# Bias rows written once and copied in memory; the last two expert tiles and the final norm by token half

## What is computed

```python
def second_block(x, c, ...):                       # x is the first block's output
    mod = (silu(c) @ w_mod + b_mod)                # 6 x 1024: sh1, sc1, gt1, sh2, sc2, gt2
    h = rmsnorm(x, ln_mix_g) * (1 + sc1) + sh1
    ...                                            # attention with a relative bias:
    s = einsum('bqgrd,bngd->bgrqn', qb, kc) + head_bias(t[:, None] - cmp_end)
    ...
    x = x + gt1 * (mixed @ w_out)
    h2 = rmsnorm(x, ln_ffn_g) * (1 + sc2) + sh2
    x = x + gt2 * peer_ffn(h2, peer_wq, peer_keys, peer_u, peer_v)
    return rmsnorm(x, ln_final_g)
```

## Time and profile before

| | |
|---|---|
| median of three runs | 1329.93 us (1328.16 to 1331.64) |
| profiled execution, its own time | 1328.11 us |
| its span | 1326.2 us |
| TensorE matmul busy | 1229.8 us, 93% |
| VectorE, ScalarE, GpSimd busy | 884.4, 771.6, 562.4 us |
| mean granted TensorE clock | 0.973 |
| moved by DMA | 249.36 MB, 188 GB/s |

### The profile page before, as it was taken

The page is one execution under the profiler, slowest core; times in us unless marked ns, Lnnn a source line. Parts: engine busy times, 40 slices in busy tenths (PEclk is TensorE's granted clock), DMA queues, the critical chain, the costliest instruction groups (busy, mean ns, idle before and its releaser), DMA issues.

```text
span 1326.2 us, 27600 instructions
## 1 busy us (share of the span) xinstructions
PE 1229.8 (93%) x8788; PEld 1124.6 (85%) x8788; DVE 884.4 (67%) x1750; ACT 771.6 (58%) x1719; POOL 562.4 (42%) x501
## 2 busy tenths in 40 slices
PE   7698988988898898999999999999999999999996
PEld 6587877877796677999999999999988878888885
DVE  4377858879735644799447777773086867676765
ACT  5233576544545544655678887886555555555554
POOL 2454445353325733698886777777700000000000
PEclk8899999999998989999999999999999999999998
DMA  5666655575452433455555656566666565757552
GB/s 212 123 223 196 204 199 185 192 259 185 150 209 105 150 97 125 148 186 177 172 175 183 192 187 197 189 191 207 241 200 253 195 240 195 259 191 254 192 196 87
DMA packets 86032, 249.36 MB, mean 188 GB/s; under 512 B 8275, under 2 KB 29907, under 8 KB 85196
## 3 DMA queue, kind: packets, MB, share of 16 engines
q1 hardware_dynamic: 77212, 209.69, 47.7%
q0 software_dynamic: 8752, 38.80, 9.1%
HBM read 235.36 MB, written 13.11 MB: 187 GB/s over the span
## 4 chain that ended last, share of the span: by engine, by line
PE 76%; DVE 9%; ACT 5%; DMA 4%; issue 3%; POOL 2%; DVEq 0%; ACTq 0%; SPq 0%
PE psum L639 75%; DMA ring<-weights 2%; DVE s_sb L1580 2%; POOL arena L1512 2%; ACT w_hi L1081 1%; DMA arena<-mods 1%; DVE w_lo L1571 1%; DVE arena L1805 1%; PE psum L817 1%; ACT arena L1222 1%; DMA ring<-v_rows 1%; DVE rstd L1565 1%; DVE arena L1673 0%; DMA par<-params 0%; DVE h_lo L1608 0%
## 5 line engine op out<-in xcount | busy, mean ns | idle before, releaser
L1081 ACT ACTIVATE w_hi<-ring 128x512 fp32r<-128x512 f32 x734 | 444.6, 627 | 299.5 <-PE psum L639 271.6
L1438 POOL TENSOR_TENSOR w_lo<-ring,w_hi 128x512 fp32r<-128x512 f32 x367 | 480.9, 1320 | 304.6 <-ACT w_hi L1081 292.1
L639 PE MATMUL psum<-h_hi,w_hi 128*128 128x256 f32 x1832 | 538.0, 294 | 50.7 <-DVE w_lo L1571 16.3
L639 PE MATMUL psum<-h_lo,w_hi 128*128 128x256 f32 x1832 | 523.2, 286 | 0.0
L639 PE MATMUL psum<-h_hi,w_lo 128*128 128x256 f32 x1832 | 522.5, 285 | 0.0
L639 PEld LDWEIGHTS psum<-h_hi,w_hi 128*128 128x128 f32 x1832 | 355.8, 194 | 69.8 <-ACT arena L1064 33.4
L639 PEld LDWEIGHTS psum<-h_lo,w_hi 128*128 128x128 f32 x1832 | 356.5, 195 | 0.2
L639 PEld LDWEIGHTS psum<-h_hi,w_lo 128*128 128x128 f32 x1832 | 356.0, 194 | 0.0
L1571 DVE TENSOR_TENSOR w_lo<-ring,w_hi 128x512 fp32r<-128x512 f32 x239 | 181.0, 757 | 144.0 <-ACT w_hi L1081 143.8
L639 PE MATMUL psum<-w_hi,h_hi 128*128 128x512 f32 (+1 forms) x592 | 223.9, 378 | 6.9 <-DVE arena L1588 5.6
L639 PE MATMUL psum<-w_hi,h_lo 128*128 128x512 f32 (+1 forms) x592 | 222.6, 376 | 0.0
(11 more groups left out here) (204 smaller groups left out, 1145.3 us busy)
## 6 DMA issues: line engine op xcount, KB each, us to landing
ring<-u_t SPq DMA_DIRECT2D x128, 512.0 KB, 3.5
ring<-v_rows SPq DMA_DIRECT2D x128, 512.0 KB, 3.5
ring<-weights SPq DMA_DIRECT2D x115, 512.0 KB, 4.2
arena<-mods POOLq DMA_DIRECT2D x48, 512.0 KB, 4.8
routing_weights<-s_sb SPq DMA_DIRECT2D x32, 320.0 KB, 4.2
s_sb<-routing_weights POOLq DMA_DIRECT2D x5, 2048.0 KB, 9.7
bias_rows<-arena POOLq DMA_DIRECT2D x1, 1536.0 KB, 35.2
xres<-x_t SPq DMA_DIRECT2D x1, 1024.0 KB, 4.8
```

Of the source, the lines that this page charges most:

```text
L639: return nc.tensor.matmul(out, lhs, rhs, start=start, stop=stop, **kw)
L1081: nc.scalar.activation(w_hi[:, half, :], src, ACT.Copy).then_inc(hi_done, 1)
L1438: nc.gpsimd.tensor_tensor(w_lo[:, half, :], src, w_hi[:, half, :].bitcast(F32), ALU.subtract)\
```

## The change

Three edits. Line numbers in the order rows of the changed kernel are its own; `low` is L1606 there, `low` on GpSimd L1470, `low_act` L2043.

**1.** At dq1 GpSimd writes the 8 bias rows once (12 KB) to a new memory tensor `bias_row`; at the step dg0, a hundred microseconds later, it copies them 128 times from memory to memory. The waits on `sheet_in` move up by 16.

```diff
+                elif s == ("proj", "dg0"):
+                    pool.wait_ge(sheet_in, 16)
+                    pool.dma_start(bias_dram.rearrange("p h j -> p (h j)"),
+                                   bias_one.rearrange("a h j -> a (h j)").to_broadcast([P, HEADS * TRI])).then_inc(sheet_in, 16)
                 elif s == ("proj", "vc"):
-                    pool.wait_ge(sheet_in, 16)
+                    pool.wait_ge(sheet_in, 32)
...
                     if s[1] == "dq1":
                         pool.wait_ge(rel_read, 1)
-                        pool.dma_start(bias_dram.rearrange("p h j -> h p j"),
-                                       bias_rows.unsqueeze(1).to_broadcast([HEADS, P, TRI])).then_inc(sheet_in, 16)
+                        pool.dma_start(bias_one[0], bias_rows).then_inc(sheet_in, 16)
...
                         if p == 8:
-                            dve.wait_ge(sheet_in, 32)
+                            dve.wait_ge(sheet_in, 48)
```

```diff
+            for i in range(TT):
+                for n in (P - 2, P - 1):
+                    s, k = n % 4, NSPLIT + P + n % 4
+                    if i == 0:
+                        pe_.wait_ge(act_hi, n + 1)
+                        pe_.wait_ge(act_lo, n + 1)
+                    for b in range(2):
+                        if i == 0:
+                            pe_.wait_ge(hi_done, 2 * (NSPLIT + P + n) + b + 1)
+                            pe_.wait_ge(*((lo0_done, NSPLIT + n + 1), (lo1_done, NSPLIT + P + n + 1))[b])
+                        w1, w0 = (w[:, (2 * k + b) % 4, :] for w in (w_hi, w_lo))
+                        out, t = y_bank(i, b), slice(P * i, P * i + P)
+                        mm(out, h_hi[:, s, t], w1, False, False)
+                        mm(out, h_lo[:, s, t], w1, False, False)
+                        last = mm(out, h_hi[:, s, t], w0, False, n == P - 1)
+                last.then_inc(y_done, 1)
...
-            act_tiles(48, P)
+            act_tiles(48, P - 4)
+            for n in range(P - 4, P):
+                high_v(n % 4, n, False, (0,) if n == P - 1 else (0, 1))
+                high_act(n % 4, n, n // 2 + 1 - POOL_TILES // 2, False)
+            high_v(3, P - 1, False, (1,))
...
+                if final:
+                    low_act()
                 dve.wait_ge(hi_done, 2 * (NSPLIT + P + n) + 2)
...
+            for s in range(4):
+                low_v(s, P - 4 + s, s == 3)
```

**3.** The final norm goes by half. ScalarE squares the two pieces of half 0, takes the root for it, then the same for half 1 (`row_square`, `row_root`, now into free blocks of `arena`). VectorE:

```diff
+            def add_gated(i):
+                dve.wait_ge(y_done, P - 1 + i)
+                for b in range(2):
+                    v.tensor_tensor(y_gated[:, i, half_of(b)], y_bank(i, b), gate_row[:, half_of(b)], ALU.mult)\
                         .then_inc(y_scaled, 1)
+                if i:
+                    row_sum(0)
+                for b in range(2):
+                    dve.wait_ge(y_scaled, 2 * i + b + 1)
+                    x = x_rows[:, i, half_of(b)]
+                    v.tensor_tensor(x, x, y_gated[:, i, half_of(b)], ALU.add).then_inc(x3_ready, 1)
...
+            add_gated(0)
+            add_gated(1)
+            row_inverse(0)
+            scale_row(0)
+            row_sum(1)
+            scale_row(1)
+            row_inverse(1)
+            scale_row(2)
+            scale_row(3)
```

More of the change, by code:

```diff
@@ L1053, in _ @@
                     v_tile(s, it * 4 + s, False, False)
-            for s in range(4):
-                v_tile(s, P - 4 + s, False, s == 3)
+            for s in range(2):
+                v_tile(s, P - 4 + s, False, False)
+            for i in range(TT):
[14 more added lines that the diff above has]
+                last.then_inc(y_done, 1)
         @block.scalar
@@ L1370, in _, with high_v @@
             gelu(2, P - 2)
-            def high_v(s, n, first):
-                for b in range(2):
+            def high_v(s, n, first, halves=(0, 1)):
+                for b in halves:
                     act.wait_ge(slot_in[(NSLOT + P + s) % RING], slot_count(NSLOT + P + s, n - s))
@@ L1419, in _, with row_square, row_root @@
                     nc.scalar.activation(gate_row[:, half_of(b)], psum[:, XBANKS[b], :], ACT.Copy).then_inc(gate_row_read, 1)
-            act_tiles(48, P)
+            act_tiles(48, P - 4)
[3 more added lines that the diff above has]
+            high_v(3, P - 1, False, (1,))
             nc.scalar.activation(small[:, 60:62], eps_c[:, 0:2], ACT.Sqrt)
-            for k in range(4):
+            def row_square(k):
                 act.wait_ge(x3_ready, k + 1)
-                nc.scalar.activation(y_gated[:, k // 2, half_of(k % 2)], x_rows[:, k // 2, half_of(k % 2)], ACT.Square,
+                nc.scalar.activation(flat(28 + 2 * k, 2), x_rows[:, k // 2, half_of(k % 2)], ACT.Square,
                                      accum_out=small[:, 16 + k:17 + k]).then_inc(row_squared, 1)
-            act.wait_ge(row_ssq, 1)
-            nc.scalar.activation(small[:, 22:24], small[:, 20:22], ACT.Sqrt, scale=1.0 / D, bias=eps_c[:, 0:1])\
-                .then_inc(row_std, 1)
+            def row_root(i):
+                act.wait_ge(row_ssq, i + 1)
+                nc.scalar.activation(small[:, 22 + i:23 + i], small[:, 20 + i:21 + i], ACT.Sqrt, scale=1.0 / D,
+                                     bias=eps_c[:, 0:1]).then_inc(row_std, 1)
+            row_square(0)
+            row_square(1)
+            row_root(0)
+            row_square(2)
+            row_square(3)
+            row_root(1)
         @block.gpsimd
@@ L2002, in weigh, with low_v, low_act @@
                 v.tensor_tensor(a, a, g_back[:, 2 * k:2 * k + 2, :], ALU.mult).then_inc(weighted, 1)
-            def low_v(s, n):
+            def low_v(s, n, final=False):
+                def low_act():
+                    dve.wait_ge(act_hi, n + 1)
+                    v.tensor_tensor(h_lo[:, s % 4, :], arena[:, n, :], h_hi[:, s % 4, :].bitcast(F32), ALU.subtract)\
+                        .then_inc(act_lo, 1)
                 low(2 * (NSPLIT + P + s) % 4, ring[:, (NSLOT + P + s) % RING, 0:HSLOT], 2 * (NSPLIT + P + n) + 1)
+                if final:
+                    low_act()
                 dve.wait_ge(hi_done, 2 * (NSPLIT + P + n) + 2)
@@ L2010, in low_v @@
                                 ALU.subtract).then_inc(lo1_done, 1)
-                dve.wait_ge(act_hi, n + 1)
-                v.tensor_tensor(h_lo[:, s % 4, :], arena[:, n, :], h_hi[:, s % 4, :].bitcast(F32), ALU.subtract)\
-                    .then_inc(act_lo, 1)
+                if not final:
+                    low_act()
             WEIGH_AT = range(1, GRP, 2)
@@ L2037, in _ @@
                 low_group(j)
-            with dve.Fori(LATE * 24 // 4, P // 4) as it:
+            with dve.Fori(LATE * 24 // 4, P // 4 - 1) as it:
                 for s in range(4):
                     low_v(s, it * 4 + s)
+            for s in range(4):
+                low_v(s, P - 4 + s, s == 3)
             dve.wait_ge(xt_read, 4)
@@ L2055, in _, with row_sum @@
[L2055 to L2060, removed]
+            def row_sum(i):
+                dve.wait_ge(row_squared, 2 * i + 2)
+                v.tensor_tensor(small[:, 20 + i:21 + i], small[:, 16 + 2 * i:17 + 2 * i], small[:, 17 + 2 * i:18 + 2 * i],
+                                ALU.add).then_inc(row_ssq, 1)
```

19 lines of the change are left out of this document (8 added, 11 removed).

## The result

The changed kernel takes **1310.56 us** (median of four runs, 1307.39 to 1315.16) against 1329.05 for the kernel before beside it (1328.06 to 1331.64): a ratio of 0.9861, 95% interval 0.9845 to 0.9877, 18.5 us. The forecast was 1313.5 in a range of 1309.5 to 1319. The profiled execution is the slowest of the four: 1315.16 us, span 1312.9.

A forecast was written before the change was run, and what follows sets the result against it. TensorE, busy 93% of the span, was taken as the bound, with its standstills left to gain: 13.2 us before dv plus 3.2 at the end, 16.4, giving 1313.5 us from the median 1329.93; range 1309.5 to 1319.

The forecast's parts named there:

- The two places named: TensorE's idle and low-clock stretch from 48.0 to 63.7 us, and the end after the last matmul at 1313.51.
- The hole: Before dv: weight slot loads delayed beside the old bias write; without it dv starts earlier, 13.2 us saved (12.8 to 13.6).
- One sign: Expected in the changed profile: the span's parts after dv's first matmul moved by 13 us as a block.
- The copy: At dg0, 1536 KB memory to memory: taken as 8 us, costing nothing if ended 12 to 13 us after issue.
- the cover: Behind the dg0 copy: time before queued weight and modulation loads are needed, letting it last 12 to 13 us free.
- The rivals of 17.6 and 35 us: Copy at dg0 only twice as fast as the old write (1317.6, 12%), or no faster (1334.5, 4%).
- Why the old write was slow: Bias write at dq1, 35.2 us: 8 rows outermost, so by the skill's rule at most 8 engines.
- The 48.7%: Share of the 16 DMA engines' time held by the old write's queue from 40 to 50 us.
- The rival built on that rule alone: Copy at dg0 gains only from 8 engines becoming 16: 17.6 us, modulation loads late, 1317.6 in all; 12%.
- The loads behind the write: Weight slot loads after dq1 land in the median 4.2 us, so the one issued at 35.75 lands at about 40.
- The tail: Last two tiles: finishing token half 0 first lets VectorE begin at 1311.32, not 1314.04; 3.2 us saved with stores.
- h_lo moved ahead: Last tile: h_lo made before the lo1 subtraction on VectorE, in time for its need at 1309.66; no matmul waits.

The follow-up runs named there:

- bias_only: Kernel before with only the 12 KB write at dq1, the memory copy at dg0 and the higher counts, end untouched: 1315.26 us, ratio 0.9895.
- no_copy: Changed kernel without the copy in memory, the sheet read from the one row and the bias shift left out: 1309.84 us, ratio 0.9860.
- run 6: Changed kernel with the memory copy issued right behind the small write, at the old write's place, not at dg0: 1309.92 us, ratio 0.9858.
- run 1: The changed kernel again, unaltered, against the kernel before on the same chip: 1311.28 us against 1329.23, ratio 0.9854.

## Why the prediction was right, point by point

- **What bounds the kernel: right.** The two places named are the two that moved.
- **The hole, 13.2 us (12.8 to 13.6): right.** 13.2 to 13.4 from 45 to 75 us in every trace without the old write; bias_only timed 14.0. dv's first matmul was put at 53.7 to 54.5 and came at 52.86; 1.2 us of that was there at 45 us already, and differs from run to run (0.2 to 1.4). One sign did not come: the later parts did not move by 13 us as a block. By the table they were 13.2 us ahead at 122 and 8.4 at 600 in the profiled execution, since it spent more time at the lower clock.
- **The copy, 8 us by the reload's rate and free up to 12 or 13: right.** 8.0 us; no_copy gains nothing, and three copies put the end of the cover at 13.8. That it came out at 8.0 exactly is luck, for the rate was that of another kind of transfer, and the same copy took 7.8 to 9.6 us at dg0 in the other traces. The rivals of 17.6 and 35 us are out.
- **Why the old write was slow: the step that failed,** though no term of the sum hangs on it. The forecast put it down to the 8 rows outermost ("The 48.7% agree with it"), and to the SBUF source only in a rival. The 48.7% did show that half of the engines held it, not why it lasted 35 us. Form alone: 12.4 to 13.7 us, no hole. Eight spread partitions of another tile: 14.7 us, no hole. The eight neighbouring partitions: 35. The rival built on that rule alone, the copy at half of the old write's 35.2, took a ratio of engine counts for a ratio of times.
- **The move to dg0: costed at nothing, rightly, but without asking whether it was needed.** It was not (run 6).
- **The loads behind the write at the median of 4.2: right,** 3.4 to 3.9.
- **The tail, 3.2 us: mechanism right, size too small, 4.1.** VectorE begins 2.19 us before the last matmul's start, as worked out (1311.32 against 1313.51). Two terms were mis-sized. The last product ends 6.14 us behind that start and not 6.6: half 1 begins 0.43 after it where I had 0.53, and the second root comes early enough for the last two quarters to start 4.29 us after half 1 and not 4.66. And the stores I counted as 0.1: from the last product's end to the end of the span it is 2.46 us (1312.9 - 1310.44) where it was 3.02 (1326.2 - 1323.18), 0.56.
- **h_lo moved ahead, no gap: right.** Without the move the gap is 0.53 us, and the last 24 matmuls take 0.8 longer.
- **The sum: 2.1 us too small, in range.** By rows it is 13.3 + 4.1 = 17.4 us and not 16.4. The medians moved by 18.5, and by 18.0 in run 1. Another 0.9 us of the 2.9 between 1313.5 and 1310.56 is the kernel before, which took 1329.05 beside the changed one and not 1329.93. The profiled executions show only 12.95 (1328.11 to 1315.16), though the two terms stand in their rows: between 75 and 285 us the changed one gave back 5.5 us, and the 10.3 us more that it spent at the lower clock are most of it. Such steps come or stay away from one execution to the next; that is much of the spread of 1307 to 1315. Whether the last microsecond of the medians is chance or the change makes such steps rarer is not settled.

## What to carry to other kernels

When a small tile is written out many times, look first at where it lies: the same bytes in the same form took 35 us out of eight neighbouring partitions and 14.7 out of eight spread ones. Spread them or go by way of memory, and only then think of the write's place in the program. And a slow transfer harms by length: it held half of the engines for 35 us and the loads beside it took 21 to 27 us, while transfers of the same size in 10 to 15 us, at the same place, let them land within 10.2 us and cost TensorE at most 0.85 us. Before one profiled execution is read against another, align the same instructions at several places; a difference that comes in steps beside a lower clock is not the change's.

## What was not expected of the hardware

- 1.5 MB by GpSimd's queue to memory, in pieces of 1.5 KB out of eight partitions: 35 us from partitions 0 to 7 of one tile, 14.7 from 0, 4 to 28 of another. Out of all 128 partitions it is 11.8; from memory to memory 7.8 to 10.2 with 128 rows outermost and 12.4 to 13.7 with 8.
- Another 1.5 MB in the densest stretch of weight loads (DMA share 0.87 from 40 to 50 us in run 6) raised the slots' landing from 3.6 to 6.5 us in the median, 9.2 at most, and cost TensorE nothing.
- After the same idle time of 1.7 us the granted clock was 0.57 from 174 to 178 us in one execution and 1.00 in the other.
